# Two blocks of gates of a transformer layer computed token-major instead of feature-major, with the norm of the delta rule's output taken along rows

## The reference, cut to what matters

```python
proj = h @ w_in                       # 256 x 18464
(rq, rk, rv, rg, gqkv, ga, gb, gz, gate_a, gate_b) = split(proj)
# retention: 8 heads of 128 keys and 256 values
yr = retention_chunked(rope(rq), rope(rk), rv)
yr = (yr - mean(yr)) * rsqrt(var(yr) + 1e-5) * ret_gn_g
yr = silu(rg) * yr
# gated delta rule: 16 heads of 128, in chunks of 64 tokens
yg = gated_delta_chunked(gq, gk, gv, log_a, beta)
yg = yg * rsqrt(mean(yg * yg, axis=-1) + 1e-6) * gdn_norm_g   # one gain of 128 values
yg = silu(gz) * yg
merged = sigmoid(gate_a) * yr + sigmoid(gate_b) * yg
```

## Time and profile before

| | us |
|---|---|
| median of 3 runs | 2980.44 (2978.79 to 2981.71) |
| the profiled execution | 2979.59 |
| its span | 2977.9 |

### The profile page before, as it was taken

One profiled execution on the slowest core, in us unless ns is written; L12 is line 12 of the kernel. 1 busy time (PEld: TensorE's weight loads), 2 busy tenths in 40 slices (PEclk: granted clock), 3 DMA queues, 4 the chain that ended last, 5 costly groups with the idle time before them and its releaser, 6 DMA issues.

```text
span 2977.9 us, 40691 instructions
## 1 busy us (share of the span) xinstructions
PE 2937.1 (99%) x16770; PEld 2553.3 (86%) x16770; DVE 1969.2 (66%) x2489; ACT 1459.1 (49%) x1786; POOL 30.0 (1%) x61
## 2 busy tenths in 40 slices
PE   8999999999999999999999999999999999999998
PEld 8899888888888888888888888888888888888887
DVE  7654567678766678778778775457557555655555
ACT  5434644356443356566666663445336344444434
POOL 0000200000000000000000000000000000000000
PEclk9999999999999999999999999999999999999999
DMA  6544444564444443333333344554345555454453
GB/s 259 194 171 155 142 184 184 198 235 170 174 169 180 185 159 142 114 128 114 128 128 126 118 149 154 204 184 170 142 170 185 197 198 195 181 190 185 183 197 141
DMA packets 72376, 504.79 MB, mean 170 GB/s; under 512 B 8160, under 2 KB 8288, under 8 KB 12416
## 3 DMA queue, kind: packets, MB, share of 16 engines
q1 hardware_dynamic: 71568, 498.21, 45.3%
q0 software_dynamic: 336, 3.80, 0.3%
q10 hardware_dynamic: 288, 0.18, 0.0%
HBM read 500.06 MB, written 2.10 MB: 169 GB/s over the span
## 4 chain that ended last, share of the span: by engine, by line
PE 91%; DVE 3%; ACT 3%; issue 1%; DMA 1%; SPq 0%; ACTq 0%; DVEq 0%
PE double L1250 82%; PE bank L1250 8%; PE bank L1253 1%; ACT whi L1619 1%; DVE wlo L1957 1%; ACT L1654 0%; DMA raw<-in_wall 0%; ACT L1824 0%; DVE gz L1980 0%; DVE cacc L1963 0%; DMA vec<-in_vec 0%; DVE dM L1957 0%; DVE gz L1957 0%; ACT ecr L1824 0%; DVE acc L1957 0%
## 5 line engine op out<-in xcount | busy, mean ns | idle before, releaser
L1250 PE MATMUL double<-AA,whi 128*128 128x512 f32 (+1 forms) x6032 | 2024.9, 386 | 6.0 <-DVE wlo L1957 3.5
L1250 PE MATMUL double<-AA,wlo 128*128 128x256 f32 (+2 forms) x5648 | 1584.9, 281 | 0.0
L1250 PEld LDWEIGHTS double<-AA,whi 128*128 128x128 f32 x6032 | 1108.7, 188 | 242.2 <-DVE wlo L1957 6.0
L1619 ACT ACTIVATE whi<-raw 128x1024 fp32r<-128x1024 f32 x926 | 924.4, 1048 | 736.8 <-PE double L1250 696.1
L1957 DVE TENSOR_TENSOR wlo<-raw,whi 128x1024 fp32r<-128x1024 f32 (+1 forms) x934 | 1101.2, 1214 | 201.8 <-ACT whi L1619 199.7
L1250 PEld LDWEIGHTS double<-AA,wlo 128*128 128x128 f32 (+1 forms) x5648 | 1064.6, 189 | 2.8 <-issue 1.2
L1250 PE MATMUL double<-whi,BB 128*128 128x512 f32 x1024 | 316.9, 389 | 0.0
L1250 PEld LDWEIGHTS double<-whi,BB 128*128 128x128 f32 x1024 | 192.2, 188 | 40.3
L1980 DVE TENSOR_REDUCE tmp<-double 128x512 f32<-128x1024 f32 x76 | 93.0, 1224 | 164.6 <-PE double L1250 164.6
L1250 PE MATMUL double<-wlo,BB 128*128 128x512 f32 x512 | 199.2, 389 | 0.0
L1250 PE MATMUL double<-whi,AA 128*128 128x512 f32 x512 | 159.1, 390 | 0.4 <-DVE wlo L1957 0.4
(11 more groups left out here) (341 smaller groups left out, 2039.1 us busy)
## 6 DMA issues: line engine op xcount, KB each, us to landing
raw<-in_wall SPq DMA_DIRECT2D x462, 1024.0 KB, 4.8
raw<-in_wall SPq DMA_DIRECT2D x9, 256.0 KB, 6.7
X<-in_xT SPq DMA_DIRECT2D x1, 2048.0 KB, 11.3
Mm<-in_memT POOLq DMA_DIRECT2D x1, 2048.0 KB, 16.1
mblk<-in_memT SPq DMA_DIRECT2D x8, 256.0 KB, 5.6
out<-XT SPq DMA_DIRECT2D x8, 256.0 KB, 2.9
dec<-in_dec POOLq DMA_DIRECT2D x1, 1536.0 KB, 9.3
hs<-in_hsT SPq DMA_DIRECT2D x4, 272.0 KB, 5.8
```

What stands on the lines that cost most here:

```text
L1250: return q.matmul(out, lhsT, rhs, start=start, stop=stop, skip_group_check=True)
L1619: q.activation(whi[j % SPL][:, c], raw[j % RAW][:, c], ACT.Copy).then_inc(S("w_hi"), 1)
```

## The change

The pairs rg and gta (4 each of 512 features instead of 8 of 256) and gz and gtb (likewise) become kind N. In the delta stage an even `h` has the gz pair and an odd `h` the gtb pair, each for two `h` at once, so every `h` keeps its 10 units. The gates are read by `ts1` with the factor of each token; the sigmoid and the products take two tiles each.

In the retention stage the gate is multiplied onto `yn` before the transposition (new step `rgt` on DVE), and the transposed result is scaled by its gain by ACT.

In the delta stage `g_o` exchanges stationary and moving operand, so the output of a chunk lies on 64 partitions by 256 columns. ACT squares it in four pieces of 128 columns with a sum along the row (`accum_out`), Ln and Exp run on 4 columns; DVE multiplies norm and gate at once in four pieces (`g_end`); PE transposes (new step `g_tr`), and DVE multiplies by the gain and adds to `Mixed` in one instruction. `g_end` waits in the plan until the gates of its two `h` exist. The hooks that start the memory's norm at `h` = 7 are moved into the four units of the last gtb pair.

```diff
-        for i in range(2):
-            add("rg", 2 * h + i, "w_in_2", 4096 + 512 * h + 256 * i)
-        for i in range(2):
-            add("gta", 2 * h + i, "w_in_2", 14368 + 512 * h + 256 * i)
+        add("rg", h, "w_in_2", 4096 + 512 * h, nu=4, kt=4, nc=512)
+        add("gta", h, "w_in_2", 14368 + 512 * h, nu=4, kt=4, nc=512)
...
-        add("gz", h, "w_in_2", 12320 + 256 * h)
-        add("gtb", h, "w_in_2", 16416 + 256 * h)
+        if h % 2 == 0:
+            add("gz", h // 2, "w_in_2", 12320 + 512 * (h // 2), nu=4, kt=4, nc=512)
+        else:
+            add("gtb", h // 2, "w_in_2", 16416 + 512 * (h // 2), nu=4, kt=4, nc=512)
...
+    def ev_token_gate(stage, then):
+        def f(tag, h, bs, full):
+            a, b = tmp.take(), tmp.take()
+            ts = (a[0], b[0])
+            tmp.held.update(ts)
+            r = evac(stage, h, bs, full, t=ts, tf=(a[1], b[1]), sig=up("sig", 2))
+            tasks.append(g_gate(stage, h, ts, then))
+            return emptied(r)
+        return f
+
+    def g_gate(stage, h, ts, then):
+        yield
+        r = add(stage + "_in", h, t=ts, g=up("gated", 2))
...
+        yield
+        if then:
+            tasks.append(then(h))
...
+    def g_rtr(h):
+        while h not in normed:
+            yield
+        add("rgt", h, v=up("ret_vec", 4))
+        yield
+        for e in range(2):
+            b, bf = side.take()
+            r = add("rtr", (h, e), b=b, bf=bf, full=up("ret_pe"), m=up("ret_m", 2))
+            side.free(b, "ret_m", r["m"])
+            yield
...
         t, tf = tmp.take()
-        tmp.held.add(t)
-        add("g_sq", h, t=t, tf=tf, a=up("gdn_act"))
+        r = add("g_nrm", h, t=t, tf=tf, a=up("gdn_act", 6))
+        tmp.free(t, "gdn_act", r["a"] - 2)
+        yield
+        while h // 2 not in gates:
+            yield
+        add("g_end", h, v=up("gdn_vec", 4))
         yield
         b1, f1 = side.take()
-        r = add("g_nrm", h, t=t, b=b1, bf=f1, p=up("gdn_pe"), a=up("gdn_act", 2))
...
-        r = add("g_end", h, t=t, v=up("gdn_vec", 2), m=up("gdn_m"))
+        r = add("g_tr", h, b=b1, bf=f1, p=up("gdn_pe"), m=up("gdn_m"))
+        side.free(b1, "gdn_m", r["m"])
+        ended.add(h)
         yield
...
-                o = bank[r["b1"]][:, g * 64:(g + 1) * 64]
+                o = bank[r["b1"]][rows, g * 128:(g + 1) * 128]
                 if ch:
-                    mm_group(o, S_[:, g, :], qg[s][:, 2 * g + t_, rows], start=True, stop=False)
-                ins = mm_group(o, vn[rows, g, :], qkt[s][rows, 2 * g + t_, rows], start=not ch, stop=True)
+                    mm_group(o, qg[s][:, 2 * g + t_, rows], S_[:, g, :], start=True, stop=False)
+                ins = mm_group(o, qkt[s][rows, 2 * g + t_, rows], vn[rows, g, :], start=not ch, stop=True)
...
-        def s_g_nrm(h, r):
+        def s_g_tr(h, r):
             free(r["bf"])
-            q.wait_ge(S("gdn_act"), at["g_sq", h]["a"])
-            mm_group(bank[r["b"]][:, :], C("ones"), tmps[r["t"]][:, :]).then_inc(S("gdn_pe"), 1)
+            q.wait_ge(S("gdn_vec"), at["g_end", h]["v"])
+            for g in range(2):
+                for t_ in range(2):
+                    ins = transpose(bank[r["b"]][:, g * T + t_ * 128:g * T + (t_ + 1) * 128], ob[:, t_, g * 128:(g + 1) * 128])
+            ins.then_inc(S("gdn_pe"), 1)
...
+            for k in range(4):
+                c = slice(k % 2 * 128, (k % 2 + 1) * 128)
+                q.activation(tmps[r["t"]][:, k * 128:(k + 1) * 128], ob[:, k // 2, c], ACT.Square,
+                             accum_out=osum[:, k:k + 1]).then_inc(S("gdn_act"), 1)
+            q.wait_ge(S("gdn_act"), r["a"] - 2)
+            rsqrt(ors[:, :], osum[:, :], 1.0 / 128, C("eps6"), "gdn_act", r["a"])
...
+        def by_token(out, r):
+            for m, x in enumerate(halves(r)):
+                ins = ts1(out(m), x, ftok[:, m:m + 1], ALU.mult)
+            ins.then_inc(S("ev"), 1)
...
+        def s_rgt(h, r):
+            q.wait_ge(S("gated"), at["gta_in", h]["g"])
+            q.wait_ge(S("ret_vec"), at["rn", h]["v"])
+            for k in range(4):
+                y, c = yn[:, k, :], slice(k // 2 * 256, (k // 2 + 1) * 256)
+                tt(y, y, Gt[h % 2][:, k % 2, c], ALU.mult).then_inc(S("ret_vec"), 1)
...
         def s_g_end(h, r):
             q.wait_ge(S("gdn_act"), at["g_nrm", h]["a"])
...
+            q.wait_ge(S("gated"), at["gtb_in", h // 2]["g"])
+            for k in range(4):
+                o = ob[:, k // 2, k % 2 * 128:(k % 2 + 1) * 128]
+                c = h % 2 * 256 + k % 2 * 128
+                stt(o, o, ors[:, k:k + 1], gz[k // 2][:, c:c + 128], ALU.mult, ALU.mult).then_inc(S("gdn_vec"), 1)
+
+        def s_g_tr(h, r):
+            q.wait_ge(S("gdn_pe"), r["p"])
             m = flat(Macc2[:, 2 * h:2 * h + 2, :])
-            tt(m, m, o, ALU.add).then_inc(S("gdn_m"), 1)
+            stt(m, bank[r["b"]][:, :], V("gdn_norm_g_2", 0), m, ALU.mult, ALU.add).then_inc(S("gdn_m"), 1)
```

More of the change, by code:

```diff
@@ L647, in g_gab @@
         yield
[L649 to L660, removed]
+    def ev_token_gate(stage, then):
[10 more added lines that the diff above has]
+        r = add(stage + "_in", h, t=ts, g=up("gated", 2))
+        tmp.free(ts[0], "gated", r["g"] - 1)
+        tmp.free(ts[1], "gated", r["g"])
+        yield
+        if then:
+            tasks.append(then(h))
     def ev_rv(tag, h, bs, full):
@@ L703, in make_plan @@
         pair("N", "rv", phase3, ev_rv)
[L704 to L707, removed]
+        pair("N", "rg", phase3, ev_token_gate("rg", None))
+        pair("N", "gta", phase3, ev_token_gate("gta", g_rtr))
     def ev_gab(tag, j, bs, full):
@@ L755, in g_conv, with gate_done @@
         P.at["got", ("qk"[n], h)] = ("cnv_vec", r["y"])
-    def ev_gz(tag, h, bs, full):
-        t, tf = tmp.take()
-        tmp.held.add(t)
[L760 to L770, removed]
-        tmp.held.add(t)
-        tasks.append(g_gate("gtb", h, t))
-        return emptied(evac("gtb", h, bs, full, t=t, tf=tf, sig=up("sig")))
+    gates, ended = set(), set()
+    def gate_done(h):
+        gates.add(h)
+        return iter(())
+    ev_gz_all, ev_gtb_all = ev_token_gate("gz", None), ev_token_gate("gtb", gate_done)
+    def ev_gz(tag, h, bs, full):
+        assert not h or 2 * h - 1 in ended
+        return ev_gz_all(tag, h, bs, full)
     def g_gdn(h):
@@ L861, in make_plan, with loads @@
             add("diag", 0, t=td, tf=f, v=up("nrm_vec", 2))
[L862 to L871 removed]
+            u = done["unit"]
+            def loads():
+                for n in range(2):
+                    add("load_mb", n)
+                b, f = side.take()
+                r = add("rmem", 0, t=td, b=b, bf=f, full=up("nrm_pe"), c=up("nrm_vec"))
+                tmp.free(td, "nrm_pe", r["full"])
+                side.free(b, "nrm_vec", r["c"])
+            first_mem = {(u + 2, 0): loads, (u + 3, 0): lambda: memn(range(4), u + 3)}
+        pair("N", "gtb", phase3, ev_gtb_all, half=True, lazy=h == 7, hooks=first_mem if h == 7 else {})
     for n in range(2, 8):
@@ L1235, in program @@
     RET_END = P.n["ret_m"]
-    gdn_end = at["g_end", 7]["m"]
+    gdn_end = at["g_tr", 7]["m"]
     def tensor_program(q):
```

163 lines of the change are left out of this document (72 added, 91 removed).

## The result

The changed kernel takes 2975.44 us (median; 2972.79 to 2976.68), the kernel before 2980.59 (2978.79 to 2981.89) on the same chip. The ratio is 0.9982, 95% interval 0.9975 to 0.9989: faster by 5 us, a quarter of the forecast 21, and outside the range of 2949 to 2971. The profiled execution of the changed kernel takes 2973.03 us. The executions of each of the two differ by 3 to 4 us among themselves.

A forecast was written before the change was run, and what follows sets the result against it. PE, busy 2937.1 of 2977.9 us, was taken to bound the kernel. Terms -10.6 - 4.1 + 0 - 7.5 + 1.5 = -20.7 gave 2958.9 us against the profiled execution, 2959.7 on the median; range 2949 to 2971.

The forecast's parts named there:

- Step 1: Retention and delta stages: 64 units of rg, gta, gz and gtb go from kind T to N, 0.165 us each, -10.6 us.
- rival B: Main matmuls: time follows columns, not instructions, so the units' change of kind gives 0; 2970.3 us, chance 7%.
- Step 2: Delta stage norm: the matmul with ones goes, four transpositions come; eight times 0.51, -4.1 us.
- Step 3: Delta stage, g_o with operands exchanged: one more change of form in 24 chunks against faster loading, 0 (-2.4 to +2.2) us.
- Step 4: Delta stage: PE's waits for the square of ob go and those for TT mostly go, -7.5 us (-3.7 to -9.5).
- step 5: Delta stage: new waits, mainly PE at g_tr for DVE's g_end, which waits for ACT; +1.5 us (0 to +8).
- Rival D: Delta stage: g_tr becomes PE's wait once for each h, as DVE stands for ACT's table loads; slower, 2999.7 us, chance 5%.
- The edits costed at nothing: Gate reading, retention's rgt and scalings, the seam to the delta stage, SP's loads, temporaries: all taken as covered, 0 us.
- A: PE's work shrinks by the low ends and the delta stage's stalls stay; 2969.6 us, chance 20%.

The follow-up runs named there:

- The run with the transposition: The changed kernel with one added 128 x 128 transposition directly before the first matmul of rq at h = 1, 2 and 3: 2973.9 us, ratio 0.9976.
- the kernel with both edits: The changed kernel with the retention's last transpositions begun a slot earlier and g_o's matmuls ordered by form: 2961.28 us, ratio 0.9938.

## Why the prediction was wrong, step by step

**Step 1 (64 units, -10.6): mis-sized, -5.2 measured.** Kind N does save time over kind T, so rival B falls, which put this step at nothing. The rule of the Trainium skill behind it (TensorE: Matmul & The Clock Gate, "Back-to-back issue gap"), by which the prediction estimated 1.3 us, is too low here too. But the term is half. The third window holds 30.5 of the changed units. They bring 1.9 us at full clock (the 4.0 of the left column holds 2.1 of clock), and 4.1 without the 2.2 that the entries into `g_o` cost: 0.13 each, inside the bounds. In the first three head pairs 24 units bring 1.1. There the units of kind N cost 5.57 us and not 5.445: I took the price from an unbroken stretch of four, and every piece of side work between them costs a slower start: 24 matmuls take 5.89 us behind the matmuls of rope and 5.57 behind those of the scores. (Kind T pays there as well: 32 matmuls took 6.05 and 5.63.) The removed units of kind T cost 5.66. That difference, 24 x 0.087 = 2.1, is then halved by what the step never considered: rq and rk, not changed at all, lose 0.33 us in each of three head pairs, since they now stand behind kind N. The run with the transposition gives 0.3 back in each, so it is what stands between N and T that does it. In the second window, with 9.5 of the units, the matmuls of the units take the same 93.5 us as before: the low clock behind the wait eats the gain. In the kernel with both edits, where it is missing, they take 92.3. The prediction's own sign ("if retention gains under 0.5 us for each `h`, step 1 was wrong") was met: it gained 0.36.

**Step 2 (norm, -4.1): right.** -3.5.

**Step 3 (`g_o`, 0, bounds -2.4 to +2.2): wrong, +7.7 measured.** The step that failed most. I counted one more change of form in 24 chunks, at 0.09. In fact there are two more, at 0.14 each: into `g_o`, where `qg` was of the units' form before, and from `qkt` to `kd`. A chunk costs 0.09 us more on the unit's matmul in front of it, 0.18 up to `kd` and 0.05 in it (24 x 0.32 = 7.7). The price was low because 0.36 against 0.27 in the earlier trace rows shows only what a change adds in front of it, not the 0.05 behind it; the count was low because I looked at the forms inside the chunk and not at the one it is entered from. What I set against it, 0.1 us a chunk for loading 64 columns, brought nothing that shows.

**Step 4 (stalls, -7.5): right, with step 5.** The waits in the third window fall by 6.4 at full clock (7.3 between the two profiled executions); forecast were -7.5 and +1.5, so -6.0. The rows for `TT` and the squares are gone as predicted. That the sum fits so well is in part luck: 9.5 us of named waits went and not 7.5, and others came (those for "issue"), which no step had. The squares followed each other every 0.30 us, the low bound.

**Step 5 (new waits, +1.5): the mechanism is there once.** PE waits 1.0 us for `ob` once, in the last `h`. Rival D did not come.

**The edits costed at nothing: one was wrong, +4.4 measured.** I wrote that half a unit covers the last `rtr` at the seam, and looked at what waits for `rtr`: POOL's clearing. I did not look at what `rtr` itself waits for. Its new step `rgt` is on DVE, and DVE's queue holds `gab1` before it, which waits for three table loads: 3 x 1.28 us. The kernel before has these loads at the same place (its chain has them from 1085.19 to 1089.56); there DVE's product came behind PE's transposition and so could not hold it. The 1.28 us of a load agree with the Trainium skill (ScalarE: Activation LUTs, "What ACT_TABLE_LOAD costs"). The page adds 1.38 us of drain for every switch to another set of functions, and these rows don't show it: the loads start 1.54 us apart with a function of 0.23 between.

**The sum.** Forecast -20.7, measured in the profiled executions -6.6. The gap of 14.1 is 5.4 (step 1), 7.7 (step 3), 4.4 (seam), 1.2 (clock ahead of the changed code) and 0.6 for step 2, less 3.8 (clock in the third window of the kernel before), 0.4 for waits, 0.8 for other side matmuls and 0.2 behind the last window. None of the rivals was it, though the times of A and B (2969.6 and 2970.3) lie nearer to the measured one than the forecast: A leaves the stalls, which went, and B puts step 1 at nothing. The seam and the form changes stand in no rival.

The page of the profile had warned where to look: PE was busy 2937.1 of 2977.9 us. Three of the four mistakes (the price of kind N, rq and rk, `g_o`, the seam) are in PE's own instructions, and two of them (rq and rk, `g_o`) in instructions that the diff leaves as they are in number.

**Open.** What sets the speed of kind T (346.7 or 353.3 ns a pair) is not settled. Shown for the second block: directly behind kind N it is slow; two float32 passes don't help; one transposition makes it fast in all three places of retention and in every second of the feed-forward, or in the first alone if given there alone. In the changed kernel this holds for 11 of 12 stretches of kind T directly behind kind N. The twelfth (1074 us, 347.4 ns on average) begins with the 32 matmuls of the decay's projection, which have the form `128*32`; its pairs of the form `128*128` behind them are slow too (six pairs from 1080.06 to 1082.18 us, 353 ns each). But kind N in front is not the whole cause: the stretch of 224 behind the last transpositions of the delta stage is slow in the changed kernel, and fast in one run.

## What to carry to other kernels

A step that moves onto another engine's queue is to be read from both ends: who waits for it, and what stands ahead of it in that queue, table loads of a third engine included. When operands of small matmuls are exchanged, write down rows and columns of the stationary form for each instruction in order, with the matmuls in front and behind, count the changes, and group equal forms; it is free and here took back 6.8 us of a loss of 7.7. Before windows of two executions are compared to a microsecond, their granted clocks are to be compared: here 3.8 of 10.9 us were not the change's. The price of a kind of matmul is to be taken in the surroundings in which it will stand, for the neighbours that stay as well.

## What the runs showed of the hardware

- A change of the stationary form cost 0.14 us between float32 matmuls of 64 to 128 rows (1.44 against 1.16 us for the same eight passes in another order), 0.09 in front of it and 0.05 behind.
- A pair of 512 and 256 columns took 346.7 or 353.3 ns in nearly every long stretch of the second block, both at a granted clock of 1.00; 512 columns of kind N took 226.8 ns. One transposition of 0.11 us between the kinds could shift 256 matmuls from 45.21 to 44.46 us.
- After a wait of PE of 4.2 us pairs of matmuls ran 0.64 us apart instead of 0.35, and the wait cost 1.3 us more than its length in one kernel's profile and 2.6 in another's. Behind a wait of 1.5 us the granted clock fell in the kernel before (0.66 from 1763 to 1768 us) and stayed at 1.00 in the changed one.
